# The small attention between the halves of the input projection, and three modulation units moved into the scan

## The chip, the cores and the metric

The kernel runs on one core of a Trainium2 chip, in one launch. A core has TensorE (matmuls, weight loads), VectorE (DVE), ScalarE (ACT), GpSimd (POOL) and SyncE (SP, which here issues the weight loads); each works through its own queue in order, and they are tied together by semaphores. The time is that of the device for one launch, in microseconds (us).

## What is computed

Two blocks follow each other. The change lies in the first one: two layers over 256 tokens x and 256 context tokens xc, 1024 wide, in fp32. Cut to what matters:

```python
for i in range(2):                                   # layers
    mod, mod_c = silu(c) @ w_mod[i] + b_mod[i], silu(c_ctx) @ w_mod[i] + b_mod[i]
    h, hc = modulate(rms_norm(x), mod), modulate(rms_norm(xc), mod_c)
    u, uc = h @ w_in, hc @ w_in      # columns: q 256, kv 128, rope 32 | b, c, val 256 each | z 512, xs 512, B 128, C 128, dt 16
    # small attention: 4 heads, 64 + 32 wide keys, values 64 wide
    q = rope(rms_norm(u_q) @ w_uq);  k, v = rms_norm(u_kv) @ w_ukv (+ rope part)
    y_att = softmax(q k^T * scale) v
    y_sc  = b * dwconv(c * val)                      # short convolution
    xs, B, C = silu(dwconv(...));  dt = softplus(dt + bias);  la = -dt * exp(a_log)
    y_ssd = norm((scan(xs, B, C, dt, la) + d * xs) * silu(z))   # both directions, chunks of 128
    x = x + gate * rms_norm(concat(y_att, y_sc, y_ssd) @ w_out) # and then the feed-forward part
    # in layer 0 the same for xc; layer 1 needs xc only for keys, values and the scan's start state
```

## The kernel before

Activations lie with features on the partitions and the 512 tokens (context first) along the free dimension. A projection is a row of **units** (`fm`): 256 output columns as two halves of 128, one 1 MB weight load into one of three `raw` buffers. Each half's weights are split into a high and a low part, `whi` on ACT (L1588) and `wlo` on DVE (L2151), and 24 matmul records (three passes, L1046 to L1048) make the half. A layer's input projection has the units kv, q, bc (B and C), xs0, xs1, gc, val, gb, z0 and z1. Layer 0 works on all 512 columns; layer 1 does so for kv, bc, xs0 and xs1 and on 256 for the others. SP loads in the order of the units; a load waits until the unit three before it no longer needs its buffer.

A **modulation unit** (`mod_units`, L1094) is one load of 1 MB of `w_mod` and 16 short matmul records; ACT copies the row it gives, TensorE transposes it (L1078) and DVE reduces it (L2370). These units need nothing of the layer's work and are used as filler between steps: `filler(n, upto)` takes the next n from a list, and `FILL` says how many stand at each place in layers 0 and 1.

The list `steps` is walked by every engine in the same order, so it sets the order of the work everywhere. `s_...` are signals: one engine ticks, another waits. PSUM banks 0 to 2 rotate among units and fillers; 3 to 7 have fixed users.

The steps that the change touches: `mla_square` and `mla_norm` normalize QC and CK (sums on TensorE L1206, L1209; DVE L2402 to L2404, L2485, L2490). `mla_proj` is the query projection (L1220), keys (L1225) and values (L1229), their copies on ACT (QT L1872, KT L1875, VV L1878, the rotated key part L1881) and the rotation of QT on DVE (L2500 to L2503). `mla_att` i is one of a staggered row of steps: scores of item i (L1252), transposes of item i-2 (L1241), product with V for a pair of items (L1261). An item is a head in one part of the tokens: 8 in layer 0, 4 in layer 1. `ssd_dt` makes LA from dt (DVE L2546 to L2561), `ssd_cs` its cumulated sums, `ssd_tok` transposes XC to XTK. Then the **scan**: `ssd_head` for 8 heads (L1328 to L1332), every two followed by their products (L1345), the recurrence `ssd_rec` on DVE (L2614, L2616) after head 1, and w_out's units. In this kernel the whole attention stands by itself behind z1, in layer 0 with a modulation unit after each of its first seven steps:

```python
        steps.append(("mla_proj", l))
        att = [(l, 2 * p + e, sg) for p in range(MLA_HEADS // 2) for sg in ((0, 1) if l == 0 else (1,)) for e in (0, 1)]
        for i in range(len(att) + 3):
            steps.append(("mla_att", att, i))
            if i < MLA_FILLED:
                filler(*FILL["mla"][l])
```

## Time and profile before

| | us |
|---|---|
| median of three runs (lowest, highest) | 1649.65 (1649.46, 1651.49) |
| the profiled execution: time, span | 1653.87, 1652.1 |
| TensorE, DVE, ACT busy | 1530.2, 985.0, 911.5 |
| layer 0: attention and its fillers (176.8 to 216.4) | 39.6 |
| layer 0: scan, up to the norm (216.4 to 292.9) | 76.5 |
| layer 1: attention (832.2 to 855.6) | 23.4 |

A line of a timeline gives start, duration, engine, line of the kernel, operation, output and inputs, shapes and how many instructions it stands for, and in brackets the idle time before it with what ended it. Durations of matmuls overlap one another, so what a row of them takes is read from the starts. The granted clock is TensorE's, 1.00 being 2.4 GHz; it has a second level of 1.2 GHz.

### The profile page before, as it was taken

How to read it: one execution, taken by the hardware profiler on the slowest of the kernel's cores; microseconds unless marked ns; L12 is line 12 of the kernel's file. 1: busy time of each engine (PE TensorE's matmuls, PEld its weight loads, DVE VectorE, ACT ScalarE, POOL GpSimd, SP SyncE). 2: the span in 40 equal slices, each digit the busy share in tenths (PEclk: the TensorE clock that was granted, in tenths of full speed). 3: DMA queues.
4: the chain of work that ended last, by engine and by line, in shares of the span. 5: the costliest groups of instructions: out<-in, count | busy, mean ns of one | idle time of the engine just before them, and what ended most of it. 6: DMA issues, size and time to landing. Idle time of an engine off the chain costs nothing.

```text
span 1652.1 us, 25531 instructions
## 1 busy us (share of the span) xinstructions
PE 1530.2 (93%) x10131; PEld 1281.4 (78%) x10131; DVE 985.0 (60%) x1579; ACT 911.5 (55%) x1506; POOL 71.6 (4%) x106
## 2 busy tenths in 40 slices
PE   5999988979999999979988899998999999888887
PEld 3687445748888888838855799998999999888787
DVE  2463568484343434474767766667776767577555
ACT  5653656463241323454565655556786868377745
POOL 3000023000000000000002000000000000001200
PEclk9999889989999999999987999999999999999899
DMA  7731435332523232342316566553644434343332
GB/s 248 231 102 51 153 128 180 127 128 77 178 80 99 101 103 99 110 131 83 123 31 200 179 210 198 194 190 128 217 147 154 154 128 154 103 153 105 100 102 77
DMA packets 223639, 225.38 MB, mean 136 GB/s; under 512 B 8234, under 2 KB 222064, under 8 KB 223472
## 3 DMA queue, kind: packets, MB, share of 16 engines
q1 hardware_dynamic: 222816, 223.63, 41.9%
q8 instruction: 80, 1.31, 0.3%
q14 instruction: 39, 0.32, 0.1%
q0 software_dynamic: 704, 0.12, 0.0%
HBM read 222.68 MB, written 1.05 MB: 135 GB/s over the span
## 4 chain that ended last, share of the span: by engine, by line
PE 75%; DVE 12%; ACT 10%; issue 2%; DMA 1%; SPq 0%; POOL 0%; DVEq 0%; ACTq 0%; POOLq 0%
PE bank L1046 21%; PE bank L1048 21%; PE bank L1047 21%; PE bank L1094 2%; ACT SH L1724 2%; ACT whi L1588 1%; DVE wlo L2151 1%; PE bank L1252 1%; PE bank L1412 1%; DVE AP L2715 1%; PE bank L1440 1%; PE bank L1367 1%; ACT AP L2005 1%; DMA raw<-in_w_out_dram 1%; PE bank L1345 1%
## 5 line engine op out<-in xcount | busy, mean ns | idle before, releaser
L2151 DVE TENSOR_TENSOR wlo<-raw,whi 128x1024 fp32r<-128x1024 f32 (+2 forms) x322 | 388.2, 1209 | 260.0 <-ACT whi L1588 255.2
L1588 ACT ACTIVATE whi<-raw 128x1024 fp32r<-128x1024 f32 (+2 forms) x322 | 336.0, 1046 | 273.2 <-PE bank L1048 251.4
L1046 PE MATMUL bank<-HH,whi 128*128 128x512 f32 (+2 forms) x640 | 245.8, 384 | 18.3 <-DVE HL L2173 15.2
L1047 PE MATMUL bank<-HL,whi 128*128 128x512 f32 (+2 forms) x640 | 241.7, 378 | 0.0
L1048 PE MATMUL bank<-HH,wlo 128*128 128x512 f32 (+2 forms) x640 | 241.4, 377 | 0.0
L1046 PE MATMUL bank<-HA,whi 128*128 128x256 f32 x576 | 166.1, 288 | 13.5 <-DVE LA L2173 5.2
L1047 PE MATMUL bank<-LA,whi 128*128 128x256 f32 x576 | 163.0, 283 | 0.0
L1048 PE MATMUL bank<-HA,wlo 128*128 128x256 f32 x576 | 162.9, 283 | 0.0
L1046 PEld LDWEIGHTS bank<-HH,whi 128*128 128x128 f32 (+1 forms) x640 | 120.8, 189 | 47.9 <-issue 16.6
L1048 PEld LDWEIGHTS bank<-HH,wlo 128*128 128x128 f32 (+1 forms) x640 | 120.9, 189 | 23.5 <-issue 0.5
L1047 PEld LDWEIGHTS bank<-HL,whi 128*128 128x128 f32 (+1 forms) x640 | 121.2, 189 | 22.6 <-issue 0.9
L1046 PEld LDWEIGHTS bank<-HA,whi 128*128 128x128 f32 x576 | 111.6, 194 | 17.3 <-issue 11.5
L1047 PEld LDWEIGHTS bank<-LA,whi 128*128 128x128 f32 x576 | 111.6, 194 | 0.0
L1048 PEld LDWEIGHTS bank<-HA,wlo 128*128 128x128 f32 x576 | 111.2, 193 | 0.0
L1046 PE MATMUL bank<-FH,whi 128*128 128x512 f32 x256 | 100.3, 392 | 0.0
L1047 PE MATMUL bank<-FL,whi 128*128 128x512 f32 x256 | 99.7, 389 | 0.0
L1048 PE MATMUL bank<-FH,wlo 128*128 128x512 f32 x256 | 99.6, 389 | 0.0
L1046 PE MATMUL bank<-HX,whi 128*128 128x256 f32 x320 | 91.0, 284 | 4.0 <-DVE HXL L2173 3.9
L1047 PE MATMUL bank<-HXL,whi 128*128 128x256 f32 x320 | 90.0, 281 | 0.0
L1048 PE MATMUL bank<-HX,wlo 128*128 128x256 f32 x320 | 90.0, 281 | 0.0
L1046 PE MATMUL bank<-YH,whi 128*128 128x256 f32 x264 | 77.8, 295 | 4.5 <-DVE YL L2867 4.4
L1724 ACT ACTIVATE SH<-bank 32x512 f32<-32x512 f32 (+1 forms) x116 | 67.5, 582 | 16.7 <-PE bank L1048 15.2
(375 smaller groups left out, 3141.8 us busy)
## 6 DMA issues: line engine op xcount, KB each, us to landing
raw<-in_w_ff_dram SPq DMA_DIRECT2D x64, 1024.0 KB, 5.4
raw<-in_w_mod_dram SPq DMA_DIRECT2D x48, 1024.0 KB, 5.3
raw<-in_a_w_in_dram SPq DMA_DIRECT2D x40, 1024.0 KB, 5.1
raw<-in_w_in_dram SPq DMA_DIRECT2D x18, 1024.0 KB, 5.4
raw<-in_b_w_in_dram SPq DMA_DIRECT2D x9, 1024.0 KB, 5.3
raw<-in_w_out_dram SPq DMA_DIRECT2D x8, 1024.0 KB, 5.3
raw<-in_ple_w_gate_dram SPq DMA_DIRECT2D x8, 1024.0 KB, 5.2
raw<-in_a_w_out_dram SPq DMA_DIRECT2D x4, 1024.0 KB, 5.1
```

Of the source, the lines that this page charges most:

```text
L1046: nc.tensor.matmul(o, wh, xh, start=start, stop=False, skip_group_check=shared)
L1047: nc.tensor.matmul(o, wh, xl, start=False, stop=False, skip_group_check=shared)
L1048: return nc.tensor.matmul(o, wl, xh, start=False, stop=stop, skip_group_check=shared)
L1094: ins = nc.tensor.matmul(b[32 * q:32 * q + 32, 0:256], cs[:, k, :], raw[u.id % RAW_SLOTS][:, k * 256:k * 256 + 256], start=turn == 0, stop ...
L1252: nc.tensor.matmul(b[:, 0:nk], QT[0:QK, h, q0:q0 + P], KT[0:QK, h, 0:nk], start=True, stop=True)\
L1345: ins = nc.tensor.matmul(b[64 * e:64 * e + 64, c * P - t0:c * P - t0 + P], w[:, c, f:f + 64], of[(2 * p + e) % 4][:, ts_], start=w is XTK, ...
L1367: nc.tensor.matmul(b[:, 0:t[1] - t[0]], ones, SQ[k % 2][:, t[0]:t[1]], start=k == 0, stop=k == KC - 1)\
L1412: ins = nc.tensor.matmul(dst[e][:, g * n:(g + 1) * n], q_, k_[:, 0:n], start=True, stop=True)
L1440: ins = nc.tensor.transpose(b[:, to:to + P], att_p(ip, e)[:, src:src + P], ident)
L1588: f(whi[h % HALF_SLOTS][:, 0:n], raw[u.id % RAW_SLOTS][:, (h % 2) * n:(h % 2) * n + n], ACT.Copy)\
L1724: ins = f(SH[sh_turn[0] % 2][32 * q:32 * q + 32, 0:n, :], b[32 * o:32 * o + 32, 0:n, :], ACT.Copy)
L2151: v.tensor_tensor(wlo[h % HALF_SLOTS][:, 0:n], raw[u.id % RAW_SLOTS][:, (h % 2) * n:(h % 2) * n + n], whi[h % HALF_SLOTS][:, 0:n].bitcast( ...
```

## The change

The attention has no stretch of its own any more. Its query and key projections run between the halves of xs1, its values between the halves of gc, and its steps before, between and behind the halves of val, gb, z0 and z1. `ssd_cs` is cut in two: its first part now stands in gc's unit. `mla_square` and `mla_norm` move up by one unit. Two heads' keys share a bank. In layer 1 the C part of bc is made for x's half of the columns only, with what follows from it. The product with b is taken from PSUM, so its copy GB is gone. Buffers have new homes, so that those of the attention don't lie on those of the units around it. Of layer 0's fillers, seven in the attention become four behind val, gb, z0 and z1, and heads 1, 3, 5 and 7 get a second one; one fewer is left for the second feed-forward part.

```diff
 FILL = {
-    "mla": ((1, (1, 8)), (0, (1, 24))),
+    "win": ((1, (1, 8)), (0, (1, 24))),
+    "odd": ((1, (1, 8)), (0, (1, 24))),
     "g": ((1, (1, 8)), (1, (1, 20))),
     "head": ((1, (1, 8)), (1, (1, 20))),
     "out": ((1, (1, 8)), (1, (1, 20))),
 }
-MLA_FILLED = 7
...
-    (QT, KT, VV), o = region(R3, [("QT", [P, MLA_HEADS, T]), ("KT", [P, MLA_HEADS, T]), ("VV", [P, 4, 256])])
-    (PR0, PR1, PT0), o2 = region(o, [("PR0", [P, T]), ("PR1", [P, T]), ("PT0", [P, 4, SEQ])])
-    (PT1,), o3 = region(o2, [("PT1", [P, 4, SEQ])])
-    assert o3 <= R4
-    (ROT,), _ = region(o, [("ROT", [P, 4, SEQ])])
...
-    (ZS, XC, dtT), o = region(R5, [("ZS", [P, 4, T]), ("XC", [P, 6, T]), ("dtT", [P, T])])
+    (ZS,), _ = region(R5, [("ZS", [P, 4, T])])
+    (GC, TPW), o = region(R5, [("GC", [P, 2, T]), ("TP", [P, 2, 520])])
+    XC_AT = (o + 63) // 64 * 64
...
-    (QC, CK, KR, GC, GB, CV0, CV1), o = region(U0, [("QC", [P, 2, T]), ("CK", [P, T]), ("KR", [P, T]), ("GC", [P, 2, T]), ("GB", [P, 2, T]), ("CV0", [P, T]), ("CV1", [P, T])])
-    (XP0, XP1, TP), o = region(o, [("XP0", [P, 2, 258]), ("XP1", [P, 2, 258]), ("TP", [P, 2, 2, 258])])
+    (QC, CK, KR, QT, KT), U1 = region(U0, [("QC", [P, 2, T]), ("CK", [P, T]), ("KR", [P, T]), ("QT", [P, MLA_HEADS, T]), ("KT", [P, MLA_HEADS, T])])
+    (CV0, CV1, XP0, XP1), _ = region(U1, [("CV0", [P, T]), ("CV1", [P, T]), ("XP0", [P, 2, 258]), ("XP1", [P, 2, 258])])
+    (VV, PR0, PR1), _ = region(U1, [("VV", [P, 4, 256]), ("PR0", [P, T]), ("PR1", [P, T])])
+    (PT0, PT1), _ = region(U0, [("PT0", [P, 4, SEQ]), ("PT1", [P, 4, SEQ])])
+    (ROT,), _ = region(U0, [("ROT", [P, 4, SEQ])])
+    TP = TPW[:, :, 0:516].rearrange("p j (s t) -> p j s t", s=2)
...
     def w_in_units(l, opening):
         t1 = ALL if l == 0 else X
         w, x = A["w_in"][l], ("h", l, "mix")
         for u in opening:
             steps.append(("unit", u))
-        fm(w, 0, COL_XBC + 512, 256, two, "win", (l, "bc"), x, [ALL] * 2)
-        fm(w, 0, COL_XBC, 256, two, "win", (l, "xs0"), x, [ALL] * 2)
+        att = [(l, 2 * p + e, sg) for p in range(MLA_HEADS // 2) for sg in ((0, 1) if l == 0 else (1,)) for e in (0, 1)]
+        def at_half(part, *here):
+            if part != "z1":
+                steps.append(("split_to", 2 * next_sid() + 1))
+            for step in here:
+                steps.append(step)
+        def win(col, part, t, *here):
+            fm(w, 0, col, 256, two, "win", (l, part), x, t, (lambda: at_half(part, *here)) if here else None)
+        def step(i):
+            return ("mla_att", att, i)
+        win(COL_XBC + 512, "bc", [ALL, t1])
         steps.append(("mla_square", l))
-        fm(w, 0, COL_XBC + 256, 256, two, "win", (l, "xs1"), x, [ALL] * 2)
+        win(COL_XBC, "xs0", [ALL] * 2)
         steps.append(("mla_norm", l))
-        fm(w, 0, COL_GC, 256, two, "win", (l, "gc"), x, [t1] * 2)
-        fm(w, 0, COL_VAL, 256, two, "win", (l, "val"), x, [t1] * 2)
+        win(COL_XBC + 256, "xs1", [ALL] * 2, ("mla_q", l), ("mla_k", l))
         if l == 0:
             steps.append(("consts",))
         steps.append(("ssd_dt", l))
-        fm(w, 0, COL_GB, 256, two, "win", (l, "gb"), x, [t1] * 2)
-        fm(w, 0, COL_Z, 256, two, "win", (l, "z0"), x, [t1] * 2)
-        steps.append(("ssd_cs", l))
+        win(COL_GC, "gc", [t1] * 2, ("mla_v", l), ("ssd_cs", l, 0))
+        steps.append(("ssd_cs", l, 1))
+        steps.append(step(0))
+        win(COL_VAL, "val", [t1] * 2, step(1))
+        filler(*FILL["win"][l])
+        steps.append(step(2))
         steps.append(("short_conv", l))
-        fm(w, 0, COL_Z + 256, 256, two, "win", (l, "z1"), x, [t1] * 2)
+        win(COL_GB, "gb", [t1] * 2, step(3))
+        filler(*FILL["win"][l])
+        steps.append(step(4))
+        win(COL_Z, "z0", [t1] * 2, step(5))
+        filler(*FILL["win"][l])
+        steps.append(step(6))
+        if l == 0:
+            win(COL_Z + 256, "z1", [t1] * 2, step(7), step(8))
+            filler(*FILL["win"][l])
+            steps.append(step(9))
+            steps.append(step(10))
+            for n in range(5):
+                steps.append(("ssd_tok", l, n))
+        else:
+            win(COL_Z + 256, "z1", [t1] * 2, ("ssd_tok", l, 0), ("ssd_tok", l, 1))
+            for n in range(2, 5):
+                steps.append(("ssd_tok", l, n))
...
-        steps.append(("mla_proj", l))
-        att = [(l, 2 * p + e, sg) for p in range(MLA_HEADS // 2) for sg in ((0, 1) if l == 0 else (1,)) for e in (0, 1)]
-        for i in range(len(att) + 3):
-            steps.append(("mla_att", att, i))
-            if i < MLA_FILLED:
-                filler(*FILL["mla"][l])
-            for n in {len(att) - 1: (0, 1), len(att): (2,), len(att) + 1: (3, 4)}.get(i, ()):
-                steps.append(("ssd_tok", l, n))
...
             filler(*FILL["head"][l])
+            if h % 2 == 1:
+                filler(*FILL["odd"][l])
...
+            if u.kind == "win" and u.key[1] == "gb":
+                return ((s_sc, (u.key[0], bi)),)
...
+        def mla_k(l):
             pe.wait_ge(s_mla_n, s_mla_n.at((l, "kv")))
-            for h in range(MLA_HEADS):
-                b = acquire(3 + h, (s_kt, (l, h)))
-                nc.tensor.matmul(b[0:NOPE, 0:T], w_ukv[:, h * P:h * P + NOPE], CK, start=True, stop=True)\
-                    .then_inc(*s_mla_k.tick((l, h)))
+            for p in range(MLA_HEADS // 2):
+                b = acquire(3 + p, (s_kt, (l, 2 * p + 1)))
+                for e in (0, 1):
+                    h = 2 * p + e
+                    ins = nc.tensor.matmul(b[NOPE * e:NOPE * e + NOPE, 0:T], w_ukv[:, h * P:h * P + NOPE], CK, start=True, stop=True)
+                ins.then_inc(*s_mla_k.tick((l, 2 * p), (l, 2 * p + 1)))
+        def mla_v(l):
...
+            if part == 0:
+                pe.wait_ge(s_la, s_la.at(l))
+                b = acquire(5, (s_cs_tok, l))
+                for d in (0, 1):
+                    ins = nc.tensor.matmul(b[:, 32 * d:32 * d + 32].rearrange("p (c h) -> p c h", c=4), tri[:, d, :],
+                                    LA[:, :, 8 * d:8 * d + 8], start=True, stop=True)
+                ins.then_inc(*s_ssd_a.tick((l, "cs")))
+                return
...
-                for c in range(CHUNKS):
+                for c in range(t_of(l)[0] // P, CHUNKS):
...
+                if part == "z0":
+                    act.wait_ge(s_sc, s_sc.at((l, 1)))
...
-            act.wait_ge(s_gemm, s_gemm.at(("blk", last_win[l], 1)))
...
+                elif part == "gb" and u.packed:
+                    y = YM[:, 2:4, SEQ:T]
+                    v.tensor_tensor(y, y, both(bank(u, 1)), ALU.mult).then_inc(*s_sc.tick((l, 0), (l, 1)))
+                elif part == "gb":
+                    for bi in (0, 1):
+                        y = YM[:, 2 + bi, :]
+                        v.tensor_tensor(y, y, bank(u, bi), ALU.mult).then_inc(*s_sc.tick((l, bi)))
...
-                v.tensor_copy(GT[:, g, :], banks[5 + 2 * g]).then_inc(*s_gt.tick((l, g)))
+                v.tensor_copy(GT[:, g, t0:T], banks[5 + 2 * g][:, t0:T]).then_inc(*s_gt.tick((l, g)))
...
-                    ins = v.tensor_copy(CTd[64 * d:64 * d + 64, g, :], XC[64 * g:64 * g + 64, 5, :])
+                    ins = v.tensor_copy(CTd[64 * d:64 * d + 64, g, t0:T], XC[64 * g:64 * g + 64, 5, t0:T])
...
-                    nc.gpsimd.memset(XP1, 0.0)
-                    nc.gpsimd.memset(TP, 0.0).then_inc(*s_pads.tick(l))
+                    nc.gpsimd.memset(XP1, 0.0).then_inc(*s_pads.tick(l))
+            elif kind == "unit" and args[0].kind == "win" and args[0].key[1] == "xs0":
+                l = args[0].key[0]
+                pool.wait_ge(s_parts, s_parts.at((l, "mix", KC - 1)))
+                nc.gpsimd.memset(TPW, 0.0).then_inc(*s_tp_pads.tick(l))
```

On TensorE, at the end of the sums of `mla_norm` in layer 0, the kernel before goes on with units (bank3 and bank45 hold the sums, L1046 to L1048 are a unit's passes):

```order
L1048 MATMUL bank0<-HH_95,wlo1_57 128x512
L1206 MATMUL bank3<-RSM_109,ones_sb_62 128x512
L1209 MATMUL bank45<-SQM_108,ones_sb_62 128x512 x2
L1046 MATMUL bank1<-HH_95,whi2_54 128x512
L1047 MATMUL bank1<-HL_96,whi2_54 128x512
```

Now the sums stand one unit earlier, and xs1's first half (its last three rows are shown) is followed by the query and key projections:

```order
L1078 MATMUL bank0<-HH_95,whi0_52 128x512
L1079 MATMUL bank0<-HL_96,whi0_52 128x512
L1080 MATMUL bank0<-HH_95,wlo0_56 128x512
L1252 MATMUL bank3<-QC_150,w_uq_sb_77 96x512 x2
L1252 MATMUL bank45<-QC_150,w_uq_sb_77 96x512 x4
L1252 MATMUL bank67<-QC_150,w_uq_sb_77 96x512 x2
L1261 MATMUL bank3<-CK_151,w_ukv_sb_78 64x512 x2
L1261 MATMUL bank45<-CK_151,w_ukv_sb_78 64x512 x2
```

The projections have moved ahead of xs1's second half, and the keys have two banks' worth of rows instead of four.

On DVE, around the same place, before, QC's normalization is followed by splits of four halves of weights and then dt's chain:

```order
L2490 SCALAR_TENSOR_TENSOR QC_156<-QC_156,VT0_74,RSM_109 128x512 x2
L2151 TENSOR_TENSOR wlo1_57<-raw2_51,whi1_53 128x1024
L2151 TENSOR_TENSOR wlo2_58<-raw0_49,whi2_54 128x1024
L2151 TENSOR_TENSOR wlo3_59<-raw0_49,whi3_55 128x1024
L2151 TENSOR_TENSOR wlo0_56<-raw1_50,whi0_52 128x1024
L2243 TENSOR_TENSOR TP_165<-bank0,GC_159 128x2x256
L2243 TENSOR_TENSOR TP_165<-bank1,GC_159 128x2x256
L2803 TENSOR_SCALAR sinks8_sb_92<-sinks_sb_91 128x16
L2546 TENSOR_TENSOR XR_140<-bank45,dt_bias_sb_88 128x64
```

Now the rotation of QT, a split and two convolutions stand there ahead of dt's chain (XR):

```order
L2558 SCALAR_TENSOR_TENSOR QC_150<-QC_150,VT0_74,RSM_101 128x512 x2
L2211 TENSOR_TENSOR wlo3_59<-raw1_50,whi3_55 128x1024
L2568 STREAM_SHUFFLE ROT_164<-QT_153 32x256 x4
L2569 TENSOR_TENSOR ROT_164<-ROT_164,axial_sb_66 32x1024
L2570 TENSOR_TENSOR QT_153<-QT_153,axial_sb_66 32x4x256
L2571 TENSOR_TENSOR QT_153<-QT_153,ROT_164 32x4x256
L2576 COPY small_94<-small_94 1x1
L2211 TENSOR_TENSOR wlo0_56<-raw2_51,whi0_52 128x1024
L2420 TENSOR_SCALAR CV0_155<-XP0_157,VT0_74 128x512
L2421 SCALAR_TENSOR_TENSOR CV0_155<-XP0_157,VT0_74,CV0_155 128x512
L2422 SCALAR_TENSOR_TENSOR CV0_155<-XP0_157,VT0_74,CV0_155 128x512
L2420 TENSOR_SCALAR CV1_156<-XP1_158,VT0_74 128x512
```

Two splits are left between QC and the convolutions of xs1, the rotation stands between them, and dt's chain follows the convolutions directly.

On TensorE in the scan of layer 0, before, heads 1 and 2 (each beginning with the matmul of CST and sel_r into bank67) have the transposes of the unit before and one modulation unit (raw, silu_c_wide) between them:

```order
L1328 MATMUL bank67<-CST_169,sel_r_71 128x512
L1331 MATMUL bank3<-CST_169,sel_r_71 128x512
L1332 MATMUL bank3<-tri_neg_r_68,ident_r_73 128x512
L1331 MATMUL bank45<-CST_169,sel_r_71 128x512
L1332 MATMUL bank45<-tri_neg_r_68,ident_r_73 128x512
L1078 MATMUL bank2<-ident_sb_61,mod_row0_85 128x128 x2
L1094 MATMUL bank0<-raw0_49,silu_c_wide_84 32x256 x8
L1328 MATMUL bank67<-CST_169,sel_r_71 128x512
L1331 MATMUL bank3<-CST_169,sel_r_71 128x512
L1332 MATMUL bank3<-tri_neg_r_68,ident_r_73 128x512
L1331 MATMUL bank45<-CST_169,sel_r_71 128x512
L1332 MATMUL bank45<-tri_neg_r_68,ident_r_73 128x512
```

Now heads 1 and 2 have two between them:

```order
L1368 MATMUL bank67<-CST_168,sel_r_71 128x512
L1371 MATMUL bank3<-CST_168,sel_r_71 128x512
L1372 MATMUL bank3<-tri_neg_r_68,ident_r_73 128x512
L1371 MATMUL bank45<-CST_168,sel_r_71 128x512
L1372 MATMUL bank45<-tri_neg_r_68,ident_r_73 128x512
L1110 MATMUL bank2<-ident_sb_61,mod_row0_85 128x128 x2
L1126 MATMUL bank0<-raw0_49,silu_c_wide_84 32x256 x8
L1110 MATMUL bank1<-ident_sb_61,mod_row1_86 128x128 x2
L1126 MATMUL bank2<-raw1_50,silu_c_wide_84 32x256 x8
L1368 MATMUL bank67<-CST_168,sel_r_71 128x512
L1371 MATMUL bank3<-CST_168,sel_r_71 128x512
L1372 MATMUL bank3<-tri_neg_r_68,ident_r_73 128x512
```

The second unit after head 1 has moved ahead of head 2.

## Rows read from the trace of the kernel before

**Rows 1.** The page: the chain that ended last, shares of the span by engine.

```profile
PE 75%; DVE 12%; ACT 10%; issue 2%; DMA 1%; SPq 0%; POOL 0%; DVEq 0%; ACTq 0%; POOLq 0%
```

**Rows 2.** Stretches: busy us (instructions) by engine, granted clock, DMA share, GB/s.

```profile
176.80:216.40 39.60, 38.53 (x271) 22.14 (x271) 21.67 (x72) 24.46 (x61) 0.00 (x0) 0.87 0.57 186
216.40:292.90 76.50, 64.53 (x466) 38.64 (x466) 62.12 (x106) 45.66 (x111) 24.21 (x18) 0.89 0.51 166
...
832.20:855.60 23.40, 21.47 (x101) 12.53 (x101) 12.10 (x33) 14.72 (x30) 0.00 (x0) 0.79 0.00 1
```

**Rows 3.** TensorE timeline, layer 0, end of xs1: start, us, [idle before <-releaser].

```profile
101.83 0.39 PE L1048 MATMUL bank<-HH,wlo 128*128 128x512 f32 x1
102.06 1.02 PE L1206 MATMUL bank<-RSM,ones_sb 128*128 128x512 f32 x2
102.92 1.88 PE L1209 MATMUL bank<-SQM,ones_sb 128*128 128x512 f32 x4
104.23 0.79 PE L1046 MATMUL bank<-HH,whi 128*128 128x512 f32 x1
```

**Rows 4.** DVE timeline, layer 0, after xs1: a convolution, and QC normalized.

```profile
103.41 0.75 DVE L2353 SCALAR_TENSOR_TENSOR CV<-XP,VT,CV 128x512 f32<-128x512 f32 x1
...
111.91 1.42 DVE L2490 SCALAR_TENSOR_TENSOR QC<-QC,VT,RSM 128x512 f32<-128x512 f32 x2
```

**Rows 5.** TensorE timeline, layer 0: q, k, and the first scores.

```profile
161.55 7.03 PE L1220 MATMUL bank<-QC,w_uq_sb 128*96 128x512 f32 x16
168.51 3.65 PE L1225 MATMUL bank<-CK,w_ukv_sb 128*64 128x512 f32 x8
...
176.80 2.04 PE L1252 MATMUL bank<-KT,QT 96*128 96x256 f32 x4 [2.72 <-ACT KT L1881]
```

**Rows 6.** TensorE timeline, layer 0: the last product of two heads, in two column halves.

```profile
202.41 1.95 PE L1261 MATMUL bank<-PT,VV 128*64 128x256 f32 x16
```

**Rows 7.** ACT and DVE timelines, layer 0: last copy of QT, KR's copies, end of rotation.

```profile
168.61 0.59 ACT L1872 ACTIVATE QT<-bank 96x512 f32<-96x512 f32 x1 [1.12 <-PE bank L1220]
...
174.52 2.18 ACT L1881 ACTIVATE KT<-KR 32x512 f32<-32x512 f32 x4
...
174.99 0.14 DVE L2509 COPY small<-small 1x1 f32<-1x1 f32 x1
```

**Rows 8.** ACT and DVE timelines, layer 0: table load and dt chain, XR to LA.

```profile
128.12 1.28 ACT L1903 ACT_TABLE_LOAD   x1 [3.34 <-DVE AB L2548]
129.41 0.26 ACT L1903 ACTIVATE EX<-AB 128x64 f32<-128x64 f32 x1
...
127.56 0.22 DVE L2546 TENSOR_TENSOR XR<-bank,dt_bias_sb 128x64 f32<-128x64 f32 x1
...
133.84 0.22 DVE L2561 SCALAR_TENSOR_TENSOR LA<-DT,AA 128x64 f32<-128x64 f32 x1
```

**Rows 9.** TensorE timeline, scan of layer 0: heads L1328, modulation units L1094, w_out L1046.

```profile
227.32 0.50 PE L1328 MATMUL bank<-CST,sel_r 48*128 48x512 f32 x1
...
229.49 1.07 PE L1094 MATMUL bank<-raw,silu_c_wide 128*32 128x256 f32 x16
230.49 0.50 PE L1328 MATMUL bank<-CST,sel_r 48*128 48x512 f32 x1
...
237.49 1.93 PE L1094 MATMUL bank<-raw,silu_c_wide 128*32 128x256 f32 x16 [4.77 <-DVE modT L2370]
239.35 0.79 PE L1328 MATMUL bank<-CST,sel_r 48*128 48x512 f32 x1
...
273.94 0.80 PE L1046 MATMUL bank<-HH,whi 128*128 128x512 f32 x1
```

**Rows 10.** SP's timeline, scan of layer 0: w_out's first weight load.

```profile
255.52 0.37 SPq L940 DMA_DIRECT2D raw<-in_w_out_dram  x1
```

**Rows 11.** TensorE timeline, layer 1's attention: idle before two scores.

```profile
832.16 3.75 PE L1252 MATMUL bank<-KT,QT 96*128 96x512 f32 x4 [2.72 <-ACT KT L1881]
837.40 3.78 PE L1252 MATMUL bank<-KT,QT 96*128 96x512 f32 x4 [1.48 <-ACT PR L1898]
```

114 lines of the change are left out of this document (64 added, 50 removed).

## The prediction

> **What bounds the kernel now.** I began with the profile's chain of work that ended last. TensorE holds 75% of it, DVE 12% and ACT 10% [rows 1], so TensorE's queue is the clock of this kernel and everything else counts where that queue waits. Next come the stretches around what the change moves, one row each, where two columns matter: TensorE's busy time against the length, and the clock granted to it [rows 2]. Layer 0's small attention takes 39.6 us with TensorE busy for 38.5 of them, but at a granted clock of 0.87: part of it ran at the lower of the two levels (1.2 and 2.4 GHz). The scan has 64.5 us of TensorE work in 76.5, at 0.89, with DVE busy for 62.1. Layer 1's attention runs at 0.79. Last I read the timelines of single engines for who waits for whom. Ahead of the first scores TensorE is idle for 2.72 us in both layers, for ACT's four copies of the rotated key part [rows 5, 11], and the low clock follows each time [rows 2]. What it costs is seen on one and the same piece: the 16 records of a modulation unit take 1.07 us at full clock and 1.93 in the low state, behind an idle of 4.77 us [rows 9].
>
> The profiled execution has a span of 1652.1 us and a time of 1653.87; the median of the three runs is 1649.65. The sum is made of differences from the profiled one and applied to the median; no term rests on the 4.2 us between them.
>
> **What layer 0 gives up.** (a) Idle time around the old attention: 2.72 us ahead of the scores and 39.60 - 38.53 = 1.07 in it [rows 2, 5]: -3.8. (b) The low clock in it: 0.13 x 39.6 = -5.1, if the new place runs at full clock. (c) Three of its seven modulation units go to the scan. One costs 1.0 us by its pitch (229.49 to 230.49 [rows 9]) and with its two transposes about 1.37: 3 x 1.37 = -4.1. (d) The key projection writes two heads into one bank, in its two partition halves. Alone, eight records of 512 columns take 3.65 us [rows 5]. The bounds are that and the price of the one place where two heads already alternate in two column halves, the attention's last product: 16 records of 256 columns in 1.95 us, 0.12 each, so 0.24 for 512 columns and 1.95 us for eight [rows 6]. It is the same kind of work, so I take it: -1.7, and 0 stays as the other end. The page TensorE: Matmul & The Clock Gate of the Trainium skill, Part 3 (packing), says that a weight load overlaps running matmuls only where its row group differs; the two heads of a pair share all rows, so by it part of the saving would go. The product of rows 6 shares its rows too and is fast, so the trace speaks for the gain. Together -14.7.
>
> **What layer 0 gets.** The query projection now stands between the halves of xs1. It needs QC normalized. In the kernel before, TensorE reaches the sums at T = 102.06 [rows 3] and DVE ends QC at 111.91 + 1.42 = 113.33 [rows 4], T + 11.3, behind a convolution, the key's rotation and two root refinements. DVE's order up to there is unchanged relative to the sums, only the unit ahead is xs0 instead of xs1. TensorE in that time has only the sums (102.06 to 104.23, 2.2 us [rows 3]) and xs1's first half (24 records of three-pass product at a pitch of 0.23 [rows 3], 5.5): it arrives at T + 7.7 and waits **3.6 us**, where before whole units lay between.
>
> The second new wait is `ssd_cs` part 0, moved up by four units into gc's half. Its input LA now ends a long row of work. Counted from q's start: the last copy of QT at 7.5 (6.9 of projection, 0.59) [rows 5, 7]; DVE's rotation of QT, from the end of that copy at 169.20 to 174.99: 13.3; meanwhile ACT's copies of KT and KR (four of 0.59, then 2.18) [rows 7] to 12.5, a table load of 1.28 [rows 8] and, in sizes estimated from the 0.59 of a 512-column copy, two silus, one weight split of 1024 columns and the two padded copies: 17.6; DVE's two convolutions, 2.1 each (three instructions, two of them of 0.75 [rows 4]), to 21.9; then the dt chain, XR at 127.56 to LA at 134.06: 6.5 us, with an exposed table load in it [rows 8]: 28.6. TensorE has q 6.9, k 1.9, xs1's second half 5.5, dt 0.4, gc's first half 5.5 and v 1.9: 22.2. It waits **6.4 us**, part of it already ahead of gc's first half, whose split stands in the same rows. Behind this wait are all of gc's second half and the attention. In the kernel before LA had three units of cover. So +3.6 + 6.4 = +10.0.
>
> Each of these waits is longer than the 2.72 us that brought the low clock. What one fall costs, by rows 2: 5.1 us in the attention, and 0.11 x 76.5 = 8.4 for the scan, which the timeline shows to be two falls, 4.2 each. The first fall lies under q and k, with which QT's copies and LA move: I take 4.2. The second lies partly inside the wait for LA: 2.0, between 0 and 4.2. Layer 0 up to the scan's head 0: -14.7 + 10.0 + 6.2 = **+1.5**.
>
> **Scan of layer 0.** Heads 1, 3, 5 and 7 are followed by two modulation units. A unit needs a bank that DVE's reduction of an earlier one frees, and that reduction stands in DVE's queue behind a head's work. Before, this wait held TensorE for 4.77 us, until 237.49, with heads 0 to 2 already issued (head 2 at 230.49); head 3 came at 239.35 [rows 9]. Now the second unit of head 1's pair meets it, and head 2 is still to come: one head and one unit, 230.49 - 227.32 = 3.2 us [rows 9], fall behind the wait. DVE is busy for 62.1 of 76.5 us [rows 2]; the 14 it has free give some of this back. Then w_out: its first weight load is issued at 255.52 [rows 10], when the buffer used three loads earlier is free, which now is head 6's unit instead of head 5's; it lands some 5.4 us after its issue, at about 270, and ACT and DVE split it; its product began at 273.94 [rows 9] and now does at about 277. I take **+2.8**; -1 if the 12 us of idle take all, +5 if nothing comes back. In ff2 one unit of two is gone: **-1.4**, of TensorE time that nothing covers.
>
> **Layer 1.** bc's second block has half the columns, by rows 3 half of 24 x 0.23 and a little less for fixed cost: -2.6. Idle 2.72 + 1.48 [rows 11]: -4.2. Clock 0.21 x 23.4: -4.9. Keys: -1.7. New: the QC chain with its last four operations at half width (an estimate from rows 4: T + 10.0) against sums and half a unit, 7.2: +2.8. LA: the halves of gc are some 2.9 instead of 5.5 us, so TensorE has 16.1 us of work from q's start, and the row of copies, rotation, convolutions and dt chain ends at 25.0 (3.5 shorter for q, no constants): +8.9. Two falls: 4.2, and 1.0 since most of the second lies in the longer wait. Sum -13.4 + 11.7 + 5.2 = **+3.5**. In the scan half-width copies of GT and CTd save some DVE work, mostly covered: **-0.3**.
>
> The dropped copies of gb on ACT, the new homes of the buffers and the moved memset cost nothing that a row shows: ACT is idle between copies in all these stretches.
>
> Total 1.5 + 2.8 - 1.4 + 3.5 - 0.3 = **+6.1, 1655.7 us**.
>
> The Trainium skill's page ScalarE: Activation LUTs, What ACT_TABLE_LOAD costs, counts a drain of 1.38 us behind each load of 1.28, and one such load now stands in each row of work to LA. By it the sum would be 2 x 1.4 higher, 1658.5. Rows 8 show the load at 128.12 for 1.28 and the next activation at 129.41, without a drain, so the sum leaves it out.
>
> **Rivals.** *Faster:* the moved matmuls fill the new waits without a fall of the clock. For it: TensorE comes to the first of them from long work at full clock, and rows 5 and 9 show few cases. Against: both idles of 2.72 us in rows 5 and 11 were followed by the low level. It takes off 6.2 + 5.2: 1644.3; with the scan at -1 also, 1640.5. *The same:* the LA wait in layer 1 is half as long, because ACT's order lets the padded copies pass earlier than I count, and one q fall is missing: about 1649 to 1652. *Slower by the scan:* no slack is left on DVE behind the pairs, w_out's load lands beyond 272 and the last pair of heads starts after 276: +5 there, with 1.6 us of short waits between layer 1's attention steps: 1659.5. *The pairs of keys do not run side by side* (the change does not do what it says): +3.4, 1659.1.
>
> **How the numbers follow.** Forecast 0.38, faster 0.26, the same 0.20, slower by the scan 0.10, keys 0.06. About 0.2% (3.3 us) is what a measurement of this kernel can tell from no change. The forecast's own spread reaches into the middle a little: faster 0.26, same 0.26, slower 0.48. The range goes from just below the faster rival (1643.5) to above the slower ones together (1663).
>
> **What would show it.** Right: in layer 0 TensorE idle for about 3.6 us ahead of q, waiting for DVE's QC, and about 6.4 us in all ahead of gc's first half and the LA product; a granted clock under 1 behind each; the key rows at 0.24 us a record; head 2 of the scan at 23 us behind head 0 instead of 14; w_out's load issued about 9 us later than now relative to head 0. Wrong: full clock in those stretches, or LA ready before TensorE comes for it.

## The result and the profile after

The changed kernel takes 1669.9 us (median of four runs, 1660.0 to 1675.1) against 1649.8 for the kernel before: a ratio of 1.0107, interval 1.0075 to 1.0139. A second series (after_again, below) gave 1665.5, ratio 1.0085, interval 1.0058 to 1.0112. By the ratios it is slower by 14 to 18 us (by the medians of the first series 20); I had forecast slower by 6 and a range up to 1663. Its runs also differ by 15 us among themselves. Four executions of 2188 us and more, two of the kernel before and two of later_moved, are left out everywhere.

The order of TensorE's work shows the forecast waits. Its timeline in layer 0, and then in layer 1, at the query projection, the last value product and the product with LA:

```profile
101.77 7.08 PE L1252 MATMUL bank<-QC,w_uq_sb 128*96 128x512 f32 x16 [3.16 <-issue]
108.77 1.94 PE L1261 MATMUL bank<-CK,w_ukv_sb 128*64 128x512 f32 x8
...
122.28 1.46 PE L1267 MATMUL bank<-w_ukv_sb,CK 128*128 128x256 f32 x6
124.42 0.70 PE L1267 MATMUL bank<-w_ukv_sb,CK 128*128 128x256 f32 x2 [0.68 <-DVE XR L2611]
131.62 1.04 PE L1315 MATMUL bank<-LA,tri_sb 128*128 128x32 f32 x4 [6.50 <-ACT VV L1935]
...
786.31 5.35 PE L1252 MATMUL bank<-QC,w_uq_sb 128*96 128x256 f32 x16 [2.69 <-DVE QC L2558]
791.60 1.94 PE L1261 MATMUL bank<-CK,w_ukv_sb 128*64 128x512 f32 x8
...
807.03 1.20 PE L1267 MATMUL bank<-w_ukv_sb,CK 128*128 128x256 f32 x2 [3.12 <-DVE XR L2611]
814.23 1.03 PE L1315 MATMUL bank<-LA,tri_sb 128*128 128x32 f32 x4 [6.00 <-ACT VV L1935]
```

Against [rows 5] the keys take 1.94 us instead of 3.65. The profile names no releaser for q in layer 0, but DVE ends QC at 101.67, 0.10 us ahead of it (below). TensorE is idle for 3.16 us ahead of q (forecast 3.6) and 0.68 + 6.50 ahead of the LA product (6.4); in layer 1 2.69 (2.8) and 3.12 + 6.00 (8.9). The releaser named at the LA product is ACT's copy of VV, not LA. ACT and DVE side by side show why both are late together:

```profile
100.25 1.42 DVE L2558 SCALAR_TENSOR_TENSOR QC<-QC,VT,RSM 128x512 f32<-128x512 f32 x2
...
112.43 2.19 ACT L1927 ACTIVATE KT<-KR 32x512 f32<-32x512 f32 x4
114.64 1.28 ACT L1720 ACT_TABLE_LOAD   x1
115.93 1.48 ACT L1720 ACTIVATE XC<-CV,VT 128x512 f32<-128x512 f32 x2
...
130.26 1.21 ACT L1935 ACTIVATE VV<-bank 128x256 f32<-128x256 f32 x4
...
115.25 0.14 DVE L2576 COPY small<-small 1x1 f32<-1x1 f32 x1
...
124.14 0.22 DVE L2611 TENSOR_TENSOR XR<-bank,dt_bias_sb 128x64 f32<-128x64 f32 x1
...
130.41 0.22 DVE L2626 SCALAR_TENSOR_TENSOR LA<-DT,AA 128x64 f32<-128x64 f32 x1
```

LA is ready at 130.63, 28.9 us after q's start (28.6 forecast). But the product goes into bank 5, which the last value product used, and ACT copies VV from it only at 130.26 to 131.47, behind its silus, since VV now lies where the convolutions' buffers were. The two ends are 0.8 us apart: by these rows, taking either away alone would gain under a microsecond.

The granted clock, in the stretches of the same trace (columns as in [rows 2]):

```profile
101.80:116.40 14.60, 14.60 (x49) 7.43 (x49) 6.65 (x13) 8.69 (x14) 0.00 (x0) 1.00 0.23 73
116.40:131.60 15.20, 8.04 (x37) 6.13 (x37) 10.51 (x27) 12.19 (x19) 0.00 (x0) 0.88 0.00 0
131.60:150.00 18.40, 18.38 (x74) 15.26 (x75) 6.21 (x18) 6.63 (x13) 0.00 (x0) 0.82 0.17 57
...
786.30:814.30 28.00, 18.86 (x85) 13.17 (x85) 17.11 (x39) 17.77 (x30) 0.00 (x0) 0.81 0.13 38
814.30:832.00 17.70, 17.26 (x99) 15.07 (x100) 9.36 (x24) 7.80 (x16) 0.00 (x0) 0.82 0.26 77
...
881.00:901.00 20.00, 20.00 (x120) 11.31 (x120) 7.43 (x18) 8.51 (x24) 5.26 (x8) 0.54 0.52 167
```

No fall came under layer 0's q and k (1.00), where I had put 4.2 us; it came with the wait for LA (0.88, 0.82). In layer 1 both waits have one. The last row was not foreseen: 20 us of layer 1's scan at 0.54, with TensorE busy all the time. The whole of that scan, head 0 to the last products, ran at 0.81 before and runs at 0.73 now (rows in the next section).

In the scan of layer 0 the second unit meets the wait as forecast, head 2 coming at 238.07 (head 0 at 216.00), and w_out's first load is issued at 263.61 instead of [rows 10]'s 255.52:

```profile
236.21 1.93 PE L1126 MATMUL bank<-raw,silu_c_wide 128*32 128x256 f32 x16 [4.93 <-DVE modT L2438]
238.07 0.79 PE L1368 MATMUL bank<-CST,sel_r 48*128 48x512 f32 x1
...
273.48 1.07 PE L1126 MATMUL bank<-raw,silu_c_wide 128*32 128x256 f32 x16 [2.58 <-DVE modT L2438]
...
278.01 0.50 PE L1078 MATMUL bank<-HH,whi 128*128 128x512 f32 x1
```

### The profile page after: what moved, and what is told of

Its sections match the earlier page's. It is cut to its first block, busy times and chain, and to the rows that moved or that the text cites. A ratio compares the mean times of both kernels' runs of the same rounds, so it can differ in the third digit from the quotient of the medians.

```text
span 1668.4 us, 25519 instructions
## 1 busy us (share of the span) xinstructions
PE 1533.7 (92%) x10123; PEld 1285.8 (77%) x10123; DVE 976.3 (59%) x1578; ACT 911.1 (55%) x1505; POOL 69.8 (4%) x106
## 4 chain that ended last, share of the span: by engine, by line
PE 73%; DVE 11%; ACT 10%; issue 3%; DMA 1%; POOL 1%; DVEq 0%; ACTq 0%; POOLq 0%
PE bank L1078 20%; PE bank L1080 20%; PE bank L1079 20%; PE bank L1126 2%; ACT whi L1632 2%; ACT SH L1771 2%; DVE wlo L2211 1%; PE bank L1407 1%; PE bank L1289 1%; PE bank L1452 1%; DVE AP L2784 1%; PE bank L1480 1%; PE bank L1385 1%; PE bank L1252 1%; DMA raw<-in_w_out_dram 1%
## 5 line engine op out<-in xcount | busy, mean ns | idle before, releaser
L1078 PE MATMUL bank<-HH,whi 128*128 128x512 f32 (+2 forms) x640 | 250.6, 392 | 16.6 <-DVE HL L2233 14.3
```

Source lines behind the costliest of these rows:

```text
L1078: nc.tensor.matmul(o, wh, xh, start=start, stop=False, skip_group_check=shared)
```

## How far one trace can be trusted

Two more traces of the kernel before (before_a, before_b) and a second of the changed one changed the reading of rows 2. Here are five stretches of the first trace of before, then the same of before_b: q to head 0 and head 0 to w_out of layer 0, the same two of layer 1 (the second to its last products), and the rest of layer 1's feed-forward part from the first product with its second weights on (called the feed-forward part from here on):

```profile
161.55:216.33 54.78, 50.99 (x304) 27.00 (x302) 27.18 (x84) 33.49 (x78) 0.00 (x0) 0.91 0.41 135
216.33:273.94 57.61, 47.55 (x376) 26.90 (x375) 48.26 (x81) 37.09 (x99) 24.21 (x18) 0.87 0.52 168
820.32:855.52 35.20, 30.55 (x134) 17.41 (x132) 18.82 (x49) 24.08 (x48) 0.00 (x0) 0.85 0.00 1
855.52:900.48 44.96, 38.26 (x287) 22.53 (x287) 33.27 (x63) 26.25 (x67) 15.25 (x18) 0.81 0.65 208
969.92:1130.59 160.67, 154.11 (x1352) 153.32 (x1351) 104.51 (x113) 84.63 (x104) 0.00 (x0) 0.99 0.58 190
```

```profile
160.50:211.90 51.40, 46.32 (x303) 24.87 (x301) 27.05 (x84) 33.43 (x78) 0.00 (x0) 1.00 0.44 144
211.90:270.65 58.75, 48.72 (x376) 27.61 (x375) 48.07 (x81) 37.14 (x99) 23.45 (x18) 0.85 0.51 165
819.86:853.34 33.48, 28.06 (x134) 16.77 (x132) 18.73 (x49) 24.10 (x48) 0.00 (x0) 0.95 0.00 1
853.34:898.17 44.83, 38.47 (x286) 22.83 (x286) 33.30 (x64) 26.35 (x67) 15.20 (x18) 0.81 0.64 211
967.62:1128.29 160.67, 154.11 (x1353) 153.33 (x1351) 104.50 (x113) 84.69 (x104) 0.00 (x0) 0.99 0.59 190
```

The idle of 2.72 us ahead of the scores is in both, but after it the clock fell to 0.91 over the stretch in one execution and not at all (1.00) in the other: 54.8 against 51.4 us. The low stretch there lasted 10, 3.5 and 0 us in the three traces. The 5.1 us that I had credited to the change for it was one draw: over the same stretch the three traces lose 4.9, 1.6 and 0 us by the clock. And in the changed kernel's two traces, the last two stretches:

```profile
863.48:911.92 48.44, 40.59 (x276) 22.91 (x278) 30.93 (x63) 28.32 (x69) 14.10 (x18) 0.73 0.60 196
982.18:1148.74 166.56, 160.00 (x1352) 159.22 (x1351) 104.55 (x113) 84.54 (x104) 0.00 (x0) 0.99 0.57 183
```

```profile
864.59:914.63 50.04, 40.62 (x277) 22.91 (x279) 30.72 (x63) 28.27 (x69) 14.14 (x18) 0.72 0.58 189
983.31:1144.00 160.69, 154.12 (x1353) 153.34 (x1351) 104.48 (x113) 84.64 (x104) 0.00 (x0) 0.98 0.59 190
```

1352 or 1353 matmuls of the feed-forward part take 166.6 or 160.7 us, both at 0.98 or 0.99 of the clock: nearly all are of 256 columns, and they start every 117.8 or every 113.3 ns throughout the stretch. 7 of the 17 traces used here have the long one; the changed kernel and home had both. So nothing in the change made that, and it moves single runs by 6 us. Nor is it a property of an execution: some 11 us ahead of this stretch two small transposes of a modulation unit stand among such matmuls, and in the trace of before the pace goes from 117.8 to 113.3 ns behind them (958.80), in that of the changed kernel from 113.3 to 117.8 (970.65). What picks the pace stays open.

With means over the traces at hand (three of before, two of the changed kernel), the lengths and what the forecast had for them, in us:

| stretch | before | changed | difference | forecast |
|---|---|---|---|---|
| layer 0, end of xs0 to head 0 | 123.1 | 126.5 | +3.4 | +1.5 |
| its scan, head 0 to w_out | 57.9 | 63.3 | +5.3 | +2.8 |
| w_out to layer 1's end of xs0 (ff2's unit, half of C) | 502.6 | 497.3 | -5.2 | -4.0 |
| layer 1, end of xs0 to head 0 | 79.4 | 86.3 | +6.9 | +6.1 |
| its scan, head 0 to the last products | 45.2 | 49.2 | +4.0 | -0.3 |
| from there to its feed-forward part | 69.3 | 69.5 | +0.2 | 0 |
| layer 1's feed-forward part | 160.7 | 163.6 | +3.0 | 0 |
| the rest | 520.7 | 519.3 | -1.4 | 0 |
| sum | 1558.8 | 1575.0 | +16.3 | +6.1 |

(The end of xs0 is taken in the kernel before as the sums' start less 10.92 us, xs1's two halves. What stands ahead of it in layer 0, 91.0 and 90.7 us, is left out.)

Two estimates from the same traces say what fills these differences. One is TensorE's idle time, the other the loss by the low clock, taken as half of TensorE's busy time at 0.5. Up to head 0 of layer 0 the idle time is 4.2 to 5.5 us before and 11.3 in the changed kernel, the loss 5.0, 1.7 and 0 before and 3.2 and 5.0 in the changed kernel. In layer 1 the idle time is 5.9 to 6.6 and 13.4, the loss 4.3, 1.7 and 1.7 against 5.5 and 3.7. In layer 1's scan the loss is 7.9 to 8.1 before and 11.6 in both traces of the changed kernel. So the new waits are the main part up to the heads, and the low clock is nearly all of the +4.0 of layer 1's scan.

## The experiments

Each was run beside the kernel before; ratios are to it. The series differ by more than most effects here (the kernel before had medians from 1649.8 to 1655.3 us in them), so only the ratios compare across series. The diffs are to the changed kernel unless said otherwise.

**after_again**: no edit. 

> The changed kernel once more, to see what of its trace returns. Theory 1 (the places): the waits stand in the kernel's order, so head 0 of layer 0's scan comes at 216 again, the first matmul of ff1 at 296, head 0 of layer 1's scan at 863, and the time is near 1670. Theory 2 (the clock): the waits are the same, but how long the low clock lasts behind them is not; the three other runs of this kernel had mean clocks of 0.962, 0.956 and 0.954 and times of 1660, 1670 and 1675. Then time and mean clock move together again, about 1.5 us for 0.001 of mean clock, and the stretches of low clock lie elsewhere or last otherwise (in layer 1's scan, 18 us long in the first trace). Also to be seen: whether the 256-column matmuls of layer 1's feed-forward part run at 117.8 ns each again (113.3 in the kernel before), which is worth 6 us.

1665.5 us, 1.0085 (1.0058 to 1.0112). The waits returned to 0.1 us; the low clock did not: in layer 0 it now came under q (6.8 us) and under the LA wait (7), in layer 1's scan again 20.5. Theory 1 holds for the waits. Theory 2 is right that the low stretches move, but its link between time and mean clock is weak: 1659.3 us at 0.960, 1664.8 at 0.957, 1666.3 at 0.959, 1667.1 at 0.953. The two traces differ by 5.4 us in all, and the pace of the feed-forward matmuls alone is 5.9 of them.

**fills_win**:

```diff
-    "win": ((1, (1, 8)), (0, (1, 24))),
-    "odd": ((1, (1, 8)), (0, (1, 24))),
+    "win": ((2, (1, 8)), (0, (1, 24))),
+    "odd": ((0, (1, 8)), (0, (1, 24))),
```

> The changed kernel with the four second units of the scan put back behind val, gb, z0 and z1 of layer 0 (two each): the attention's new order alone, the scan as before. Theory 1 (my sum): the scan's pairs cost 3.7 us against before and give back 4.1 + 1.4 in the attention and ff2, so this kernel pays 4.1 up to head 0, wins 3.7 in the scan: within 2 us of the changed kernel where the clock is alike, some 1665 to 1671. Theory 2 (the pairs are the cause): without them the kernel falls back to 1655 or less.

1671.0 us, 1.0134 (1.0102 to 1.0166). The scan is 57.6 us again, so the pairs do cost the scan about 5, but head 0 comes 10.7 us later for four units worth 5.5. Beside the attention's steps a pair of units waits for ACT's row copy, for the product with b on DVE (which stands behind the short convolution) and for ACT's silus of z, 4.3 us together:

```profile
173.15 0.44 PE L1110 MATMUL bank<-ident_sb,mod_row 128*128 128x128 f32 x2 [2.33 <-ACT mod_row L1820]
174.18 1.60 PE L1126 MATMUL bank<-raw,silu_c_wide 128*32 128x256 f32 x16 [0.59 <-DVE YM L2312]
...
195.54 1.07 PE L1126 MATMUL bank<-raw,silu_c_wide 128*32 128x256 f32 x16 [1.36 <-ACT ZS L1708]
```

Theory 2 falls.

**before_odd** (to the kernel before; the scan's part of the change alone):

```diff
-MLA_FILLED = 7
+MLA_FILLED = 4
...
             filler(*FILL["head"][l])
+            if h % 2 == 1:
+                filler(*FILL["odd"][l])
```

> The kernel before with the other part of the change alone: four modulation units after the attention's steps instead of seven, and a second one after heads 1, 3, 5 and 7 of layer 0's scan. Theory 1: -4.1 in the attention, +3.7 in the scan, -1.4 in ff2: 1648, and head 2 of the scan some 8 us later relative to head 0 than before. Theory 2 (the pairs are the cause of the loss, with later consequences for buffers and loads): 1655 or more.

1648.5 us, 0.9984 (0.9964 to 1.0004). From q to head 0 it takes 48.6 us (52.6 in the mean of three traces of the kernel before), the scan 62.7 (57.9), and head 2 stands 22.1 us behind head 0 (14.2): as in theory 1. The moved units are not what made the kernel slower.

**home** and **home_again**: the attention back in its own stretch, and the second units of the scan back in it.

```diff
-    "odd": ((1, (1, 8)), (0, (1, 24))),
+    "odd": ((0, (1, 8)), (0, (1, 24))),
...
-        win(COL_XBC + 256, "xs1", [ALL] * 2, ("mla_q", l), ("mla_k", l))
+        win(COL_XBC + 256, "xs1", [ALL] * 2)
...
+        win(COL_Z + 256, "z1", [t1] * 2)
+        steps.append(("mla_q", l))
+        steps.append(("mla_k", l))
+        steps.append(("mla_v", l))
+        for i in range(len(att) + 3):
+            steps.append(step(i))
+            if i < 7:
+                filler(*FILL["win"][l])
```

> The changed kernel with the attention back in a stretch of its own behind z1, with seven modulation units in it, and the normalizations back at their old places: new buffer homes, keys in pairs, C in half width and b from PSUM stay. Transposes of XC stand behind the last attention step. Theory 1 (the interleaving costs): -2.6 and -1.4 in layer 1, -1.7 twice for the keys' pairs and +0.6 for the transposes: about 1643. Theory 2 (the new homes or the halved C cost something hidden, for instance the slower 256-column matmuls of layer 1's feed-forward part): 1650 or more, with those matmuls at 117.8 ns.

> home once more: its four runs gave 1.0065, while its one trace was no longer than the kernel before's. Theory 1 (it loses by the 3.6 us that TensorE waits in layer 1 for splits behind the short convolution and by the long low clock in layer 1's scan, against 2.6 + 3.4 + 4.1 gained elsewhere): 1.000 to 1.004. Theory 2 (the first result holds): 1.005 or more.

1660.0 us and 1.0065 (1.0041 to 1.0089) from four runs, then 1653.3 and 1.0016 (0.9993 to 1.0038) from ten. The two intervals don't overlap, so a series differs from another by more than its interval says; the 14 runs, each taken against the kernel before in its own series, have a median ratio of 1.0025. I had expected 1643, a gain of 0.5%. So the small edits (keys in pairs, half of C, b from PSUM, new homes) bring no gain here that can be measured. One place where they lose is layer 1, where the product with b must follow the short convolution on DVE and the next unit's split stands behind both:

```profile
809.49 0.39 PE L1071 MATMUL bank<-HH,whi 128*128 128x256 f32 x1 [2.85 <-DVE wlo L2204]
```

**before_chalf**, **chalf_again** (to the kernel before: half of C alone) and **odd_kpair** (to before_odd: keys in pairs alone).

```diff
-        fm(w, 0, COL_XBC + 512, 256, two, "win", (l, "bc"), x, [ALL] * 2)
+        fm(w, 0, COL_XBC + 512, 256, two, "win", (l, "bc"), x, [ALL, t1])
```

```diff
-                b = acquire(3 + h, (s_kt, (l, h)))
+                b = acquire(3 + p, (s_kt, (l, 2 * p + 1)))
```

> The kernel before with one part of the change alone: in layer 1, C for x's half of the columns only (product, padded copy, convolution, silu, the heads' B C products, copies GT and CTd). In three traces of kernels with this part layer 1's scan, head 0 to the last products, took 48.4, 50.0 and 49.2 us with a granted clock of 0.72 to 0.73, against 45.0 and 0.81 in the two without it; in a fourth (fills_win) it took 43.9. Theory 1 (the shorter start of the scan shifts its waits so that the low clock lasts longer): -2.6 before head 0, the scan 48 us or more at 0.75 or less, so about 1650 to 1652, no gain. Theory 2 (it is chance, or comes from the new homes): -2.6 - 1.4, scan at 45, about 1646.

> The kernel before with C in half width, a second trace. Its first had a low clock of 20.5 us in layer 1's scan and 48.4 us for it. Theory 1 (drawn anew): 45 us is as likely. Theory 2 (the order sets it): 48 us again, with a low stretch of 17 us or more.

> The kernel before with two parts of the change: the scan's doubled modulation units (before_odd) and the keys of two heads in one bank. Theory 1: before_odd's 1648.5 less the keys' 1.7 in each layer, 1645. Theory 2 (the wait for the rotated key part's copies on ACT sets the first scores anyway, and only the idle time ahead of them grows): 1648, with more than 2.72 us of idle ahead of the first scores.

before_chalf: 1654.9 us, 1.0003 (0.9989 to 1.0017); odd_kpair: 1655.8 us, 1.0009 (0.9989 to 1.0030), against 0.9984 (0.9964 to 1.0004) without the pairs; the kernel before had 1655.3 in this series. chalf_again, one run, 1648.7, where the kernel before had 1651.5. Half of C arrives in full at layer 1's sums (-2.5 us) and is lost in the scan (48.4 and 47.3 us for 45.0); with the keys' pairs the same scan took 49.5. The keys' pairs themselves bring 0.8 us of the 1.7 in each layer when the attention stands by itself: the first scores come 14.4 instead of 15.3 us behind q, since TensorE now waits 0.54 us for a copy of KT ahead of the values, while the 2.72 us ahead of the scores stay. Neither theory had that. That the longer low clock in the scan follows from either edit is not shown: the kernel home, which has both, had 49.2 us for it once and 44.6 once.

**before_a**, **before_b**: no edit, single executions of 1648.2 and 1652.7 us, told above. 

> The kernel before once more, for a second trace. Theory 1 (how long the low clock lasts in layer 1's scan, and whether the 256-column matmuls of its feed-forward part run at 113.3 or 117.8 ns, is drawn anew in each execution): head 0 to the last products takes 45 or 48 to 50 us by chance, the feed-forward part 160.7 or 166.6. Theory 2 (the kernel's order sets it): 45.0 us with 6.8 and 10.2 us of low clock as in the first trace.

> The kernel before a third time, for the same question. Theory 1: values other than before_a's in one of the two stretches are likely. Theory 2: 45.0 us again in the scan.

For the feed-forward part and the fall under the attention theory 1 holds. For layer 1's scan the three traces of the kernel before agree (45.0, 45.9, 44.8), and those of the changed kernel do (48.4, 50.0), while home had 49.2 and 44.6: neither a fixed property nor a fair draw.

**later**: everything one unit later, to take the new waits away.

```diff
-        win(COL_XBC + 256, "xs1", [ALL] * 2, ("mla_q", l), ("mla_k", l))
+        win(COL_XBC + 256, "xs1", [ALL] * 2)
...
-        win(COL_GC, "gc", [t1] * 2, ("mla_v", l), ("ssd_cs", l, 0))
+        win(COL_GC, "gc", [t1] * 2, ("mla_q", l), ("mla_k", l))
+        win(COL_VAL, "val", [t1] * 2, ("mla_v", l), ("ssd_cs", l, 0))
+        filler(*FILL["win"][l])
         steps.append(("ssd_cs", l, 1))
         steps.append(step(0))
-        win(COL_VAL, "val", [t1] * 2, step(1))
+        steps.append(("short_conv", l))
+        win(COL_GB, "gb", [t1] * 2, step(1))
```

The other steps of the attention follow one unit later too, the last four of layer 0 behind z1.

> The changed kernel with the interleaved attention started one unit later: xs1 undivided, query and key projections between gc's halves, values and the first part of ssd_cs between val's halves, and the attention's steps shifted to match (last four of layer 0 behind z1). It takes away what TensorE waits for ahead of q (3.2 us in layer 0, 2.7 in layer 1) and ahead of LA (7.2 and 9.1 us), since DVE then ends QC while xs1's second half runs, and the dt chain starts before QT's rotation. Theory 1 (these waits and the low clock behind them are what the new order costs): head 0 of layer 0 comes 10 to 12 us earlier than in the changed kernel (216 to about 205), layer 1's stretch to head 0 is 9 to 13 us shorter, and the whole is 1642 to 1650. Theory 2 (the interleaving costs spread over many small places, banks, ACT and DVE queues): under half of that, 1658 or more.

1651.0 us, 0.9984 (0.9961 to 1.0007). The idle time ahead of q is gone, that ahead of the LA product is 0.56 and 3.21 us, and the stretches to the heads run at nearly full clock:

```profile
132.97 0.60 PE L1315 MATMUL bank<-LA,tri_sb 128*128 128x32 f32 x4 [0.56 <-ACT VV L1935]
...
804.43 0.60 PE L1315 MATMUL bank<-LA,tri_sb 128*128 128x32 f32 x4 [3.21 <-ACT VV L1935]
```

```profile
110.68:208.51 97.83, 93.30 (x477) 65.02 (x475) 47.58 (x122) 50.93 (x100) 0.00 (x0) 0.98 0.27 86
...
787.31:848.88 61.57, 54.04 (x365) 44.12 (x363) 37.24 (x88) 37.16 (x67) 0.00 (x0) 0.97 0.22 69
```

Head 0 of layer 0 comes at 208.5 (216.0 and 218.3 in the changed kernel), and layer 1's stretch from the end of xs0 is 8 to 10 us shorter. That is theory 1, somewhat smaller than it had it (10 to 12 us, 9 to 13, and 1642 to 1650 in all): the shift by one unit gives back 1.0 to 1.2%, about all that the change had lost. Some new waits come with it: 2.00 us for ACT's copy of a modulation unit's row at 155.80, and 1.1 in two small ones.

**la_late**: only the second of later's two shifts, with the steps of the attention placed as in later.

```diff
-        win(COL_GC, "gc", [t1] * 2, ("mla_v", l), ("ssd_cs", l, 0))
+        win(COL_GC, "gc", [t1] * 2)
+        win(COL_VAL, "val", [t1] * 2, ("mla_v", l), ("ssd_cs", l, 0))
```

> The changed kernel with the wait for LA taken away and the one for QC kept: query and key projections stay between xs1's halves, values and the first part of ssd_cs go between val's halves (with the attention's steps of the kernel later). Beside later, which took both away, it parts the two. Theory 1 (each wait costs its idle time and what low clock follows): the idle ahead of q, 3.2 + 2.7 us, stays, so 6 us over later and 8 to 10 under the changed kernel, ratio to the kernel before about 1.002. Theory 2 (only the wait for LA matters, the idle ahead of q is given back behind it): like later, ratio 0.998.

1665.0 us, 1.0057 (1.0029 to 1.0084): worse than either theory (1.002 and 0.998), and not as clean a test as meant. In layer 0 the wait for LA shrank to 0.57 us, but head 0 came at 215.5, only 0.5 to 2.8 us earlier: the 3.1 us of waits that come with later's order are here too, and the clock fell under q. In layer 1 the wait was 6.92 us, though LA was ready at 814.43:

```profile
809.40 1.89 PE L1267 MATMUL bank<-w_ukv_sb,CK 128*128 128x256 f32 x8
818.21 1.03 PE L1315 MATMUL bank<-LA,tri_sb 128*128 128x32 f32 x4 [6.92 <-ACT VV L1935]
...
814.20 0.23 DVE L2626 SCALAR_TENSOR_TENSOR LA<-DT,AA 128x64 f32<-128x64 f32 x1
...
811.25 1.28 ACT L1720 ACT_TABLE_LOAD   x1
812.54 1.48 ACT L1720 ACTIVATE XC<-CV,VT 128x512 f32<-128x512 f32 x2
814.05 1.06 ACT L1632 ACTIVATE whi<-raw 128x1024 fp32r<-128x1024 f32 x1
815.13 0.60 ACT L1691 ACTIVATE GC<-bank 128x512 f32<-128x512 f32 x1
815.76 1.06 ACT L1632 ACTIVATE whi<-raw 128x1024 fp32r<-128x1024 f32 x1
816.85 1.21 ACT L1935 ACTIVATE VV<-bank 128x256 f32<-128x256 f32 x4
```

It is the bank again: ACT copies VV at 816.85, behind a table load, silus, GC and two splits. A shift of the products alone does not move what ACT has queued ahead of their copies.

**l1_only** and **l0_only**: the new order in one layer, home's in the other (the condition holds home's order; it is l == 1 in l0_only). l0_only has the changed kernel's modulation units in layer 0, second ones in the scan included, l1_only has home's.

```diff
+        if l == 0:
...
+        else:
...
```

> The changed kernel with the interleaved attention in layer 1 only; in layer 0 it is in its own stretch with seven modulation units and the scan has single ones, as in home. Against home it differs in layer 1's order alone. Theory 1: from xs0's end to head 0 layer 1 took 87.2 and 85.4 us in the two traces of the changed kernel and 82.7 in home: so 3 to 5 us slower than home, 1663. Theory 2 (the order in layer 1 is free, and the time sits in the low clock by chance): within 2 us of home, 1658 to 1662, with the clock in that stretch no lower than home's.

> The changed kernel with the interleaved attention in layer 0 only; layer 1 has it in its own stretch as in home. With l1_only (1.0068) and home (1.0065) it parts the layers. Theory 1: layer 0's new order costs its waits, 7 to 9 us against home for the same number of modulation units, and the pairs give back 2 to 3: ratio 1.009 to 1.011. Theory 2 (only layer 1's order costs): 1.0065 or less.

l1_only 1665.0 us, 1.0068 (1.0049 to 1.0086); l0_only 1659.5 us, 1.0043 (1.0019 to 1.0066). Against home_again's 1.0016 the new order would cost 0.5% in layer 1 and 0.3% in layer 0, and with home's 0.2 that makes 1.0%, as the changed kernel has. Against home's first series (1.0065) it would cost nothing in either, and l0_only's 1.0043 lies in what theory 2 had for it (1.0065 or less). So how the cost is divided between the layers is not shown by the times; the traces show the waits in both (11.3 us idle up to head 0 in layer 0 of l0_only against 5.1 in home's, 13.4 in layer 1 of l1_only against 10.5).

**later_fills** (later with fills_win's edit) and **later_moved** (later with this):

```diff
-    "g": ((1, (1, 8)), (1, (1, 20))),
+    "g": ((2, (1, 8)), (1, (1, 20))),
...
-            if h % 2 == 1:
+            if h in (3, 4, 5):
```

> The kernel later with the scan's four second units back behind val, gb, z0 and z1 (two each): the interleaved order without waits, and the scan as before. Theory 1: head 0 of layer 0 comes 5.5 us later than in later (214), the scan is 6 us shorter (58 instead of 64.5): no difference, ratio 0.998. Theory 2: as in fills_win against the changed kernel (+0.3 to 0.5%), pairs of units among the projection's halves make TensorE wait for ACT's row copies (2.3 us in fills_win) and bring the low clock: ratio 1.002.

> The kernel later with the second modulation units of layer 0's scan at other places: behind the scan's first products (g) and behind heads 3, 4 and 5 instead of behind 1, 3, 5 and 7, so that head 2 is not held behind the recurrence on DVE, and the last products and w_out's first load have no second unit ahead of them. Theory 1 (the pairs' places cost the 4 to 5 us that y3 comes later): head 0 to w_out 57 to 60 us instead of 64.5, the ratio to the kernel before 0.995. Theory 2 (the scan is bound by DVE and by the low clock behind the wait for the recurrence, whatever the order): within 1 us of 64.5, ratio 0.998.

later_fills 1652.9 us, 1.0000 (0.9974 to 1.0026); later_moved 1656.7 us, 1.0024 (0.9999 to 1.0048), of which no trace is used here. Where the units stand makes no difference that can be told: later_fills lies in the middle of its two theories (0.998 and 1.002), with both inside its interval. The better places I thought to have found for the second were none; it missed both theories (0.995 and 0.998). No version was measurably faster than the kernel before: later and before_odd come nearest, both at 0.9984 with 1 inside the interval.

## Why the prediction was off

**Right:** the sign, and the two waits with their sizes (QC 3.2 and 2.7 for 3.6 and 2.8; LA 7.2 and 9.1 for 6.4 and 8.9), the keys' pairs (1.94 us for 1.95), head 2 of the scan 22.1 us behind head 0 (23), w_out's load 8.4 us later relative to head 0 (9), and that the waits are what the new order costs: later shows it. That ACT's copy of VV was as late as LA I had not seen; I counted the row of DVE and left bank 5's user out. In layer 1 the size of that wait is luck in part: LA came 26.9 us behind q's start where I had 25.0, and TensorE's own work up to there took 18.8 where I had 16.1, q alone 5.35 us with the clock low under part of it.

**Mis-sized:** the low clock. Step (b) of layer 0 took 5.1 us, and layer 1's term 4.9, as what the old place costs; three traces of it have 4.9, 1.6 and 0 us of loss in layer 0 (0.91, 0.97 and 1.00 of the stretch) and 5.3, 1.7 and 1.7 in layer 1. So the credit was about 2 + 3, half of what I had taken. On the other side I had put 6.2 and 5.2 us of loss for the falls at the new waits; by the estimate under the table the changed kernel lost 3.2 and 5.0 us in layer 0, 5.5 and 3.7 in layer 1, somewhat less. The first error made the sum 5 us too low, the second nearly 3 too high, and the stretches up to the heads came out 1.9 and 0.8 us above the forecast.

**Mis-sized:** the pairs in the scan, +2.8 for +5.3 (62.0 and 64.5 us; before_odd and odd_kpair, 62.7 and 64.1, have the same). What I gave back for DVE's free time does not come back: that is the end I had called "if nothing comes back". I had priced the shift of the heads and not the work of the four second units, 5.5 us by the 1.37 that I gave each. TensorE's busy time from head 0 to w_out goes from a mean of 47.9 us to 53.2 and 55.6, and its idle time only from 10.0 to 8.9. The low clock has a small part in it (an estimated loss of 5.5, 5.5 and 6.8 us before, 5.5 and 8.3 now).

**Failed:** "In the scan ... -0.3" for layer 1, where +4.0 came. This is the largest single miss. The term counted DVE's copies and took the clock in this scan as unchanged without a reason; the low clock cost 11.6 us there in both traces of the changed kernel and 7.9 to 8.1 in the three of before. All but one of the traces of 47 to 50 us have a low stretch of 17 us or more in this scan, those of 44 to 46 us have one of 14 or less. What decides between them stays open: it goes with no single part (half of C, keys in pairs, new order and home all had it, fills_win, l0_only, later_fills and home_again did not).

**Not foreseen:** the two paces of layer 1's feed-forward matmuls, 3 of the 16 us here, by the chance that one of two traces had the long one; and that the runs spread by more than the 3.3 us that I took for noise: the kernel before itself lay between 1647.6 and 1660.0 us in 25 runs, the changed one between 1660.0 and 1675.1 in four, so that the median of few runs lies where chance puts it.

## What to carry over

Before work is moved into the shadow of other work, follow its inputs back to the moved place and count them against what TensorE has in that time; both ends of the product count, the operand and the bank that another engine's queue must empty first. If that row is too long by some microseconds, shift by one unit: here this was worth 1.0 to 1.2%, where half of C and keys in pairs, each alone, brought nothing that could be measured. And price the low clock from several executions: a fall of one trace is a draw, not a cost of the place.

## What the runs showed of the hardware

After the same idle of 2.72 us the lower clock came for about 10, 3.5 and 0 us in three executions of one kernel, and in layer 1's scan it stayed for 20 us although TensorE was busy for 20.00 of 20.00 us. At an equal granted clock (0.98 or 0.99) the same row of matmuls of 256 columns ran at 113.3 or 117.8 ns each for 160 us on end, and the pace changed within an execution where two small transposes stood among them (958.80 in before, 970.65 in the changed kernel). The drain of 1.38 us behind a table load that the Trainium skill's page ScalarE: Activation LUTs (What ACT_TABLE_LOAD costs) counts did not show here either: the load takes 1.28 us from 114.64, and ACT's next row, two silus, starts at 115.93 in the trace of after.
